# RWKV stage: a buffer of its own for the removal matrix, products in the middle of the levels, preparation in single hops

## The reference, cut to what matters

```python
def rwkv_scan(q, d, s0, reverse, with_output):
    def step(s, inp):
        r_t, w_t, k_t, v_t, kk_t, a_t = inp
        sa = jnp.einsum('bhvk,bhk->bhv', s, -kk_t)
        s = s * w_t[:, :, None, :] + sa[..., None] * (kk_t * a_t)[:, :, None, :] + v_t[..., None] * k_t[:, :, None, :]
        return s, (jnp.einsum('bhvk,bhk->bhv', s, r_t) if with_output else None)
```

## Time and profile before

| | before |
|---|---|
| median of 3 runs | 5507.23 us (5505.22 to 5511.69) |
| profiled execution | 5503.14 us, span 5501.1 us |
| PE busy in the span | 88%, granted clock 0.93 |
| DVE, ACT, POOL busy | 39%, 24%, 8% |
| chain that ended last | PE 73%, DVE 11%, issue 7%, DMA 4%, ACT 2% |
| RWKV stage | 145 to 1371 us, eight head pairs |

### The profile page before, as it was taken

One profiled execution on the slowest core, in us unless ns is written; L12 is line 12 of the kernel. 1 busy time (PEld: TensorE's weight loads), 2 busy tenths in 40 slices (PEclk: granted clock), 3 DMA queues, 4 the chain that ended last, 5 costly groups with the idle time before them and its releaser, 6 DMA issues.

```text
span 5501.1 us, 79608 instructions
## 1 busy us (share of the span) xinstructions
PE 4847.9 (88%) x33616; PEld 2951.6 (54%) x33616; DVE 2162.8 (39%) x3808; ACT 1300.3 (24%) x2390; POOL 430.9 (8%) x384
## 2 busy tenths in 40 slices
PE   8788888887998888988888897999999997999999
PEld 2356565566655554463333454544677554544677
DVE  2355555555245462021111335453343235353333
ACT  0233333333122221010000123332232123232232
POOL 0011111110023240000000000010000000010000
PEclk9888998998998998988999897999999997999999
DMA  6000000000100104224999211023221210113221
GB/s 243 27 17 17 15 17 17 4 4 24 46 33 29 46 8 164 77 100 161 419 419 406 89 57 39 27 74 131 92 92 46 92 62 22 41 62 129 100 92 54
DMA packets 70697, 494.58 MB, mean 90 GB/s; under 512 B 8771, under 2 KB 9027, under 8 KB 29251
## 3 DMA queue, kind: packets, MB, share of 16 engines
q1 hardware_dynamic: 70342, 489.49, 22.9%
HBM read 468.47 MB, written 21.00 MB: 89 GB/s over the span
## 4 chain that ended last, share of the span: by engine, by line
PE 73%; DVE 11%; issue 7%; DMA 4%; ACT 2%; POOL 1%; SPq 0%; DVEq 0%; POOLq 0%; PEldq 0%; ACTq 0%; PEld 0%
PE ps L224 70%; DMA upper<-in_ew 4%; PE ps L227 3%; DVE upper L235 3%; DVE upper L243 2%; DVE lower L243 1%; ACT upper L282 1%; DVE lower L235 1%; DVE upper L259 1%; POOL upper L3198 1%; DVE upper L239 1%; POOL upper L1163 0%; DVE upper L251 0%; ACT lower L282 0%; DMA lower<-in_ada 0%
## 5 line engine op out<-in xcount | busy, mean ns | idle before, releaser
L224 PE MATMUL ps<-lower 128*128 128x512 f32 (+11 forms) x6384 | 1942.3, 467 | 121.0 <-issue 25.1
L224 PEld LDWEIGHTS ps<-lower 128*128 128x128 f32 (+3 forms) x6384 | 997.1, 194 | 874.8 <-issue 672.1
L224 PE MATMUL ps<-upper 64*64 64x64 f32 (+8 forms) x14096 | 938.8, 270 | 187.1 <-DVE upper L259 71.3
L282 ACT ACTIVATE upper<-ps 128x512 f32<-128x512 f32 (+6 forms) x963 | 453.8, 483 | 2063.7 <-PE ps L224 1400.0
L224 PEld LDWEIGHTS ps<-upper 64*64 64x64 f32 (+4 forms) x14096 | 662.1, 157 | 515.6 <-issue 236.6
L224 PE MATMUL ps<-lower,upper 64*64 64x64 f32 (+6 forms) x7216 | 845.7, 341 | 71.4 <-DMA lower<-in_ew 26.8
L224 PE MATMUL ps<-rounded 128*128 128x512 f32 x3072 | 719.2, 396 | 30.7 <-DVE rounded L235 23.1
L224 PEld LDWEIGHTS ps<-rounded 128*128 128x128 f32 x3072 | 582.8, 190 | 166.2 <-ACT rounded L282 26.3
L224 PEld LDWEIGHTS ps<-lower,upper 64*64 64x64 f32 (+3 forms) x7216 | 437.6, 160 | 414.1 <-issue 366.6
L224 PE MATMUL ps<-upper,lower 128*128 128x512 f32 (+5 forms) x1200 | 508.8, 572 | 27.2 <-DVE upper L235 22.0
L282 ACT ACTIVATE upper<-upper 128x768 f32<-128x768 f32 (+10 forms) x615 | 323.6, 531 | 742.2 <-POOL upper L3198 144.3
(11 more groups left out here) (78 smaller groups left out, 2156.1 us busy)
## 6 DMA issues: line engine op xcount, KB each, us to landing
lower<-in_ew SPq DMA_DIRECT2D x144, 1024.0 KB, 12.2
upper<-in_ew SPq DMA_DIRECT2D x48, 1024.0 KB, 13.7
lower<-in_b0f SPq DMA_DIRECT2D x16, 2048.0 KB, 8.5
lower<-in_b1f SPq DMA_DIRECT2D x16, 2048.0 KB, 7.7
lower<-in_ada SPq DMA_DIRECT2D x12, 2048.0 KB, 9.6
lower<-in_wrkv SPq DMA_DIRECT2D x8, 1728.0 KB, 7.6
lower<-in_b0g SPq DMA_DIRECT2D x8, 1536.0 KB, 6.4
gad<-upper SPq DMA_DIRECT2D x48, 256.0 KB, 2.0
```

What stands on the lines that cost most here:

```text
L224: return self.e.matmul(out, lhsT, rhs, start=start, stop=stop)
L282: self.e.activation(out, in_, func, bias=bias, scale=scale, accum_out=accum).then_inc(line.up(*event), 1)
```

## The change

- **Removal matrix.** It gets a buffer b.N (512 columns a direction, both chunks). tri makes it beside the small blocks, and DVE picks it right after the blocks, with the event removal; level waits for that and no longer for products. b.L shrinks to 3 x 128 columns a head. products makes what is left, 384 columns for a latent chunk and 128 for a context one, and stands after merge 3 (u = 0) and merge 4 (u = 1). turn_bk moves from after level 3 to after level 5.
- **Order of the lanes.** The step state goes into update, so a chunk is three turns. Lane 1 starts 3 turns behind in the count (5 before).
- **Preparation.** prepper becomes two generators. projector does k, then the two loras of d = 0, r, kk_norm, v, turn_v, gate, the loras of d = 1, and may run ahead of the lanes; shifts are steps of their own, in two parts. chain does the elementwise work, one hop between engines a step, renamed (sum, mid, grown, decay, beta, keys, keys2, shrunk, alpha, query, bonus). kk's square has a buffer of its own, so it no longer waits for G and P. Waits for the readers of shared buffers are set buffer by buffer. ACT's copy of v in turn_v waits for the last update of j - 2.
- **Tail.** Seven steps instead of six (ACT's part has its own), and its two PE steps use the steppers' banks.

The core of the diff:

```diff
-                for u in range(2):
-                    before = (d, j, 2 * p + u - 2) if p else (d, j - 1, 4 + u)
-                    while before[1] >= 0 and before not in stepped:
-                        yield None
-                    yield ("products", j, d, p, u)
                 for lev in range(1, 6):
                     yield ("level", j, d, p, lev)
                     yield ("merge", j, d, p, lev)
-                    if lev == 3:
-                        yield ("turn_bk", j, d, p)
+                    if lev in (3, 4):
+                        u = lev - 3
+                        before = (d, j, 2 * p + u - 2) if p else (d, j - 1, 4 + u)
+                        while before[1] >= 0 and before not in stepped:
+                            yield None
+                        yield ("products", j, d, p, u)
+                yield ("turn_bk", j, d, p)
                 yield ("corner", j, d, p)
...
+    def projector():
+        for j in range(8):
+            for i in (1, 2):
+                for kk in range(8):
+                    yield ("project", j, i, kk)
+                if i == 1:
+                    for part in range(2):
+                        yield once(("shift", j, i, part))
+                    if j:
+                        yield from until("query", j - 1, 1)
+                    yield once(("lora", j, 0, 0))
+                    yield once(("lora", j, 0, 1))
+            yield once(("shift", j, 2, 0))
+            yield from until("kk_square", j)
+            yield once(("kk_norm", j))
             for kk in range(8):
-                yield ("turn_v", j)
...
+                yield ("project", j, 0, kk)
+            yield from free(j)
+            for part in range(2):
+                yield once(("shift", j, 0, part))
+            yield once(("turn_v", j))
+            yield ("gate", j)
+            yield from until("alpha", j, 0)
+            yield once(("lora", j, 1, 0))
+            yield once(("lora", j, 1, 1))
...
+    def chain():
         for j in range(8):
+            for d in range(2):
+                yield from until("lora", j, d, 0)
+                for name in ("sum", "mid", "grown", "decay"):
+                    yield (name, j, d)
+                if d == 0:
+                    yield from until("shift", j, 1, 1)
+                    yield once(("kk_square", j))
+                    yield from until("kk_norm", j)
+                    yield ("kk_rstd", j)
+                    yield ("kk_scale", j)
+                    yield from free(j)
+                yield from until("lora", j, d, 1)
+                for name in ("beta", "keys", "keys2", None, "shrunk", "alpha", "query"):
+                    yield once((name, j, d)) if name else None
+            yield ("bonus", j)
+            yield from until("turn_v", j)
             ready.add(j)
...
+            for u in range(2):
+                for hd, e in enumerate(heads):
+                    a = alpha_at(chunk[u])
+                    last = pe.mm(ps[:, 512 * hd + 128 * u + 128:512 * hd + 128 * u + 256], ch(o.Bn[d], chunk[u])[e, :],
+                                 o.AR[d][e, a:a + 128], True, True)
             last.then_inc(team.pe.up(*use), 1)
-            banks.give(use, team.dve, "inverse", j, d, p, 0)
+            banks.give(use, team.dve, "removal", j, d, p)
...
-            pe.wait_ge(team.dve, "products", j, d, p, 1, 1)
+            pe.wait_ge(team.dve, "removal", j, d, p)
...
+            for hd in range(2):
+                v.pick(team.dve, v3(b.N[d][:, 256 * hd:256 * hd + 256], 128), strict[d], v3(ps[:, hd, 128:384], 128),
+                       *(("removal", j, d, p) if hd else ()))
```

More of the change, by code:

```diff
@@ L616, in rwkv_map @@
     b.bk = [m(512) for _ in range(2)]
-    b.L = [[v3(m(1024), 512) for _ in range(2)] for _ in range(2)]
+    b.N = [m(512) for _ in range(2)]
+    b.L = [[v3(m(768), 384) for _ in range(2)] for _ in range(2)]
+    b.square = m(768)
     b.PX = [m(512) for _ in range(2)]
@@ L650, in prepper, with once, until, free @@
-    def prepper():
-        for j in range(8):
-            while j > 1 and j - 2 not in done:
-                yield None
-            yield from prep(j)
+    ready, done, stepped, made, seen = set(), set(), set(), set(), set()
+    def once(step):
+        seen.add(step)
+        return step
+    def until(*step):
+        while step not in seen:
+            yield None
+    def free(j):
+        while j > 1 and j - 2 not in done:
+            yield None
+    def projector():
[13 more added lines that the diff above has]
+            yield once(("kk_norm", j))
+            for kk in range(8):
+                yield ("project", j, 0, kk)
[7 more added lines that the diff above has]
+            yield once(("lora", j, 1, 1))
@@ L655, in prepper @@
             ready.add(j)
     def lane(d):
-        for _ in range(5 * d):
+        for _ in range(3 * d):
             yield None
@@ L694, in tails @@
                 yield None
-            for q in range(6):
+            for q in range(7):
                 yield ("tail", j, q)
             done.add(j)
-    return turns([lane(0), lane(1), stepper(0), stepper(1), tails(), prepper()])
+    return turns([lane(0), lane(1), stepper(0), stepper(1), tails(), projector(), chain()])
 def alpha_at(cc):
@@ L1046, in prep @@
                 v.tt(P.dve, o.fac[d][:, i:i + 1], b.mid[:, s:s + 1], b.mid[:, e:e + 1], ADD, *(("mids", j, d) if i == 4 else ()))
+        elif name == "bonus":
+            v.wait_ge(slow(k, j), "keys2", j, 1)
+            v.wait_ge(P.dve, "shift", j, 2)
+            v.stt(P.dve, o.kb, o.kb, col("rk"), b.r, MUL, MUL, "bonus", j)
     def lane(name, j, d, p, *z):
@@ L1145, in rwkv_vector @@
             lane(name, *z)
-        elif name == "state":
+        elif name == "update":
             state(*z)
@@ L1210, in prep @@
         o = b.outs[j % 2]
-        if name == "project":
-            i, kk = z
-            if kk < 7:
+        if name == "shift":
+            i, part = z
+            if part:
                 return
-            if j:
+            if i == 0 and j > 1:
+                a.wait_ge(tail.dve, "out", j - 2)
+            elif i == 1 and j:
+                a.wait_ge(slow(k, j - 1), "keys2", j - 1, 1)
+            elif i == 2 and j:
                 a.wait_ge(slow(k, j - 1), "query", j - 1, 1)
-                a.wait_ge(P.dve, "mids", j - 1, 1)
-            if j > 1:
-                a.wait_ge(tail.dve, "out", j - 2)
+                a.wait_ge(P.dve, "bonus", j - 1)
             a.wait_ge(P.pe, "project", j, i)
@@ L1223, in prep @@
             a.wait_ge(P.pe, "turn_v", j)
+            if j > 1:
+                for d in range(2):
+                    a.wait_ge(k.step[d].pe, "update", j - 2, d, 5)
             a.copy(P.act, o.vtok, k.pair(("turn_v", j))[:, 0:768], "turn_v", j)
-        elif name == "kk_norm":
+        elif name == "kk_rstd":
             a.wait_ge(P.dve, "kk_max", j)
-            a.act(P.act, b.P, b.P, AF.Ln)
-            a.act(P.act, b.P, b.P, AF.Exp, "kk_rstd", j, scale=-0.5)
-        elif name == "kk_scale":
+            a.act(P.act, b.square, b.square, AF.Ln)
+            a.act(P.act, b.square, b.square, AF.Exp, "kk_rstd", j, scale=-0.5)
+        elif name == "gate":
             a.wait_ge(P.pe, "gate", j)
-            a.copy(P.act, o.g, k.pair(("kk_scale", j))[:, 0:512], "gate", j)
+            a.copy(P.act, o.g, k.pair(("gate", j))[:, 0:512], "gate", j)
         elif name == "lora":
@@ L1320, in rwkv_gpsimd @@
             g.e.tensor_copy(v3(b.X[d], 64), bc1(c["ident2"], 4)).then_inc(line.up("unit", j, d, p), 1)
[L1321 to L1324 removed]
+        elif j and name in ("grown", "keys", "keys2", "alpha", "query"):
             rwkv_products(k, g, P.pool, j, name, *z)
```

206 lines of the change are left out of this document (95 added, 111 removed).

## The result

The changed kernel takes 5404.9 us (median of four runs, 5403.3 to 5405.7) against 5506.2 for the kernel before on the same chip (5496.2 to 5511.7): a ratio of 0.982 [0.980, 0.984], 101 us less. Forecast were 5451 us, 56 less, in a range of 5385 to 5512. The sign is right and the time lies in the range, but it lies at the very edge of the forecast's own range of 5405 to 5495; the gain is nearly twice the forecast.

A forecast was written before the change was run, and what follows sets the result against it. No engine bound on average; PE was busy 122.0 of 145.8 us a period, leaving 35 us of idle and slow clock. Stages 78 + 134 + 5 x 150 + 106 + 102 = 1170, 56 less: 5451 us, range 5385 to 5512.

The forecast's parts named there:

- shift of k: Preparation, turns 124 and 125: 9.5 us of queue until lora may have the bank, 2.8 of PE work: 6.7 us idle.
- POOL's unit copy: At tri: the unit copy stands behind keys2 and another copy on POOL, DVE's pick waits for it: 3.3 us.
- wrong if steady periods are under 140: Sign of failure for the middle periods, forecast at 150 us; also wrong over 161 or if the sixth isn't short.
- the price of a steady period: Tri to tri in the middle: 110.9 us work, 26.8 idle and 12.3 slow clock, 150 in all.
- lora: Second half shares the one bank pair and waits for ACT's sigmoid with a table load: 1.4 us, 0.6 around it.
- tail, turns 149 to 158: DVE's tail, picks, shift of v, beta, corner, shift: 20.3 us in order against 10.3 of PE work; 10 us idle.
- the slower rival: DVE becomes the bound beside POOL, operations there taking longer: 8 us a period, 19 us slower, 5526 us; chance 0.10.
- the two ends: Gains of 8 us ahead of tri 0, 8 in the first period, 41 in the sixth, 14 from tri 7 on.
- The last stretch: From tri 7 to the end of RWKV: 62 turns for 81, 102 us for 116.5, 14 won.
- Level 1's wait: Level 1 waits for three picks a lane, not eight; with smaller waits of two other pairs about 5 us a period saved.
- Ahead of tri 0: Start of RWKV: k comes first, d = 0 chain runs beside projections of r and v; 8 us won, 78 us.
- The first rival: Interleaving hides more: 12 us idle and 8 slow clock, a period of 131; 151 us less, 5356; chance 0.13.

The follow-up runs named there:

- The version with one more turn: Changed kernel with one more empty turn after the wait for the tail of j - 2, in projector and chain: 5365.8 us, ratio 0.974.

## Why the prediction was right in sign and short in size

**The queues were followed rightly.** The corner copies wait behind the tail and the shift of v, and beside turn_bk behind the shift of k (3.57 and 3.55, forecast 5 and 5 to 7). DVE waits for POOL's unit copy. The short period is 110.6 (106). Tri 1 comes at 358.5 (357), by luck: tri 0 is 5.6 us late, and the period behind it 4 us shorter than forecast. And "wrong if steady periods are under 140" has come true: four take 136.1 to 136.7 and one 139.1. By its own sign the forecast had the steady periods wrong. That the total lies in the range is luck in part: the other stages came out 16 us longer than forecast and what lies behind RWKV 6 us longer than before; without these 22 us it would be 5383, outside.

**The step that failed is the price of a steady period,** 110.9 of work + 26.8 idle + 12.3 slow clock. Of these the idle time was 13.2. Work and slow clock were about right: busy time 123.4 against 123.2. By its terms:

| stall | forecast, us | measured |
|---|---|---|
| lora | 2.0 | 0.3 |
| shift of k (turns 124 to 126, in this period 172 to 174) | 6.7 | 3.8 |
| kk_norm | 2.8 | 1.0 |
| tail, turns 149 to 158 | 10 | 6.4 |
| POOL's unit copy | 3.3 | 1.2 |
| hops and the rest | 2 | 0.5 |

The lengths of the stretches were better than that. The tail's ten turns took 22.4 us for 20.3 forecast, the three with the shift of k 10.7 for 11.0 (9.5 and the lora behind them). Neither forecast length comes out of the operations that it lists: these add up to 16.8 and 8.6 us, with the five additions at 2.25 in the second, which took 0.94. So part of the fit is luck. The tail stretch idles less all the same because PE's 10.3 us of work in it took 16.0: about half of that stretch is at the half level. In a stretch whose length another engine's queue sets, slow work of PE takes the place of waiting, and is not added to it. The forecast took the stall at full clock and then added 12.3 us of slow clock to the whole period, so some 4 to 6 us were charged twice. That double count is worked out from the trace, no run isolates it. The rest of the 13.6 us, 8 to 10, lies in the stalls of the table, each priced too high by 1 to 3 us; for 1.3 of them, the additions for fac, the next paragraph shows why, the others stay open.

**Prices taken beside POOL.** The forecast took 2.25 us for the additions of fac, and gave the slower rival 8 us a period for operations that take long beside POOL. In the changed kernel the two engines hardly meet; of the rows below only the additions of 548.10 overlap a product of POOL, by 0.3 us. The same operations, from its DVE timeline:

```profile
548.10 1.11 DVE L235 TENSOR_TENSOR upper<-lower 128x1 f32<-128x1 f32 x5
...
644.38 0.35 DVE L243 SCALAR_TENSOR_TENSOR lower<-lower,upper 128x128 f32<-128x128 f32 x1
...
673.37 0.68 DVE L239 TENSOR_SCALAR upper<-upper,lower 128x768 f32<-128x768 f32 x1
...
699.92 0.94 DVE L243 SCALAR_TENSOR_TENSOR lower<-lower,upper 128x768 f32<-128x768 f32 x1
```

State's second operation takes 0.35 us where it took 1.47, keys 0.68 for 2.33, beta 0.94 for 2.13, fac 1.11 and 0.94 for 2.25. DVE's busy time fell from 76.4 to 70.5 us a period though the picks took 2.0 more (1.8 forecast). The four kinds of operation together fell by 7.9 us (15.8 in the period before from 666.84, 7.9 in the one after from 497.57), which is the whole difference. In the version with the preparation of before it stands at 77.1. So the slower rival's mechanism was real in the kernel before, and the change did the opposite of what the rival said. How much of the time won this alone is stays open; the run that was to put the additions back beside POOL didn't get them there.

**Where the gain lies.** The forecast put it at the two ends: 8 + 8 + 41 + 14, and a loss of 17 in the five periods. Measured are 3.5, 12.5, 36.6 and 3.7 at the ends, and a gain of 48 in the five. And the 41 and 36.6 are no gain of running ahead: without it RWKV is 6 us longer and the total the same.

**The last stretch,** 112.8 for 102. The forecast had work 78, idle 16 and slow clock 8. Measured are 82 of work, 25.7 of idle and 5 of slow clock, and PE idled for 25.8 before the change as well. The idle time is the term that failed. Two waits make up 11.5 us of it, one in the last tail and one of 6.41 us, up to 1266.97, ahead of PE's first work behind RWKV, and no term of the forecast is for them; the kernel before has both as well, 5.07 and 6.40. The first:

```profile
1257.77 1.08 PE L227 MATMUL ps<-lower,upper 128*128 128x128 f32 x4 [5.07 <-DVE upper L235]
```

A smaller part is the products in the middle, which the forecast said cost nothing. PE's timeline there:

```profile
1198.40 1.58 PE L224 MATMUL ps<-upper 64*128 64x256 f32 x16 [0.78 <-DVE upper L259]
1200.63 0.34 PE L224 MATMUL ps<-upper 64*64 64x64 f32 x8 [0.65 <-DVE upper L259]
...
1201.72 0.34 PE L224 MATMUL ps<-upper 64*64 64x64 f32 x8 [0.40 <-DVE upper L259]
...
1203.13 1.97 PE L224 MATMUL ps<-upper 64*64 64x64 f32 x32 [0.48 <-ACT upper L282]
```

A lane has one pair of banks. The products (1198.40) fill it, and the next level (1200.63) can't start until DVE has picked them out, with no other work to cover that. The forecast looked only at the projection's cover, not at a turn without it. But moving them back wins nothing in this stretch: with the products first it takes 115.9 us, 26.0 of them idle.

**Level 1's wait,** 5 us a period in the forecast: nothing measurable by the two runs with the products first. The products' place is worth some 26 to 33 us in all, mostly outside the steady periods; what makes it so wasn't taken apart.

**Ahead of tri 0,** 83.0 for 78: PE idles for 20.6 us there and stands at a clock of 0.80. The shift of k is on time (159.7 for 159), the shift of v ends 5.4 us late (196.4 for 191), and query is done at 218.2 for 217. The rest is a wait of 4.38 us at 225.96, where the lora of j = 1 waits for the second part of the shift of k; it stands ahead of tri 0, and the forecast has no term for that wait.

**The first rival** (12 us of idle, 8 of slow clock, a period of 131) was nearer to the steady periods than the forecast: idle 13.2, slow clock 11.9 us (24 at the half level), a period of 136.6; it had a chance of 0.13. The version with one more turn has that rival's numbers, 128.0 and 131.5, but that engines running ahead during one stall pay for the next is not what that run tests.

## What to carry to other kernels

When a period is summed up, first say of each stretch which engine's queue sets its length; idle time and slow clock are charged only in stretches that PE itself sets, never both on the same microseconds. Price an operation both beside the engine that it disturbs and alone, and ask whether the change makes them meet; and when work is moved ahead, sum all stages before calling a short one a gain. In a schedule of turns, look for the longest waits of PE and move what stands ahead of them in the releaser's queue by one turn: that was worth 39 us here. And when an order is put back to see what it was worth, look whether the mixed kernel has a wait that neither of the two had, as the bare tails here.

## What the runs showed of the hardware

Two kernels with nearly the same idle time in a period, 13.2 and 11.9 to 12.3 us, stood at granted clocks of 0.91 and of 0.95 to 0.99. The one has waits of 3.55 and 3.57 us, the other none above 2.2, and PE is busy for 4 to 8 us less with the same matmuls. A third, with the lanes of before, idled for 14.6 us with no wait over 3.23 and stood at 0.87. So periods of like idle time differ by 8 us and more in slow matmuls, and neither the sum of the idle time nor its longest wait tells by how much.

After the change DVE's second operation of a state took 0.35 us (644.38) and beta 0.94 (699.92) with POOL idle, and before it 1.47 and 2.13 beside POOL's products. The Trainium skill (SBUF — State Buffer, "Who interferes with whom") says that a DVE operation with two inputs in SBUF contends with a GpSimd one that reads SBUF, and that the lock is exclusive. The trace of before agrees: the operation of 1.47 us ended at 630.6, 0.1 us behind the product of POOL that had started ahead of it.
